# Two experts at fixed places read ahead of routing, a late w_mod batch and five row buffers in a two-layer MoE trunk on one core

## What is computed

```
cs  = silu(c)
mod = cs @ w_mod[i] + b_mod[i]                 # w_mod (2, 1024, 6144)
sh1, sc1, g1, sh2, sc2, g2 = split(mod, 6)
h = rmsnorm(x)*(1+sc1) + sh1
mix = pool_mixer(h)        if i == 0           # windows 2, 4, 8, 16
mix = recurrent_block(h)   if i == 1           # conv of width 4, RG-LRU
x = x + g1 * mix
h2 = rmsnorm(x)*(1+sc2) + sh2
x = x + g2 * moe(h2)       # 16 experts, best group of 4, then its top 2
# moe: silu(h2 @ w_gate[e]) * (h2 @ w_up[e]) * gate, @ w_down[e]; D_FF = 512
y = rmsnorm(x)             # after both layers
```

## Time and profile before

| what | us |
|---|---|
| median of 3 runs | 1042.4 |
| the profiled execution | 1042.29 |
| its span | 1040.5 |
| TensorE busy, share | 867.1 (83%) |
| VectorE busy | 297.9 (29%) |
| ScalarE busy | 199.0 (19%) |
| GpSimd busy | 61.8 (6%) |
| SP's DMA queue, share of 16 engines | 66.3% |
| mean HBM rate over the span | 304 GB/s |

### The profile page before, as it was taken

One profiled execution on the slowest core, in us unless ns is written; L12 is line 12 of the kernel. 1 busy time (PEld: TensorE's weight loads), 2 busy tenths in 40 slices (PEclk: granted clock), 3 DMA queues, 4 the chain that ended last, 5 costly groups with the idle time before them and its releaser, 6 DMA issues.

```text
span 1040.5 us, 14093 instructions
## 1 busy us (share of the span) xinstructions
PE 867.1 (83%) x5770; PEld 446.4 (43%) x5770; DVE 297.9 (29%) x672; ACT 199.0 (19%) x355; POOL 61.8 (6%) x142
## 2 busy tenths in 40 slices
PE   2778777999999998359999999964599999999930
PEld 0433433443333332248887888743244333333210
DVE  2494470110010110363320256065110110010018
ACT  1230511000110000231111851262110000010014
POOL 1000010000011000000000000000101000011000
PEclk9989688999999999659999999967599999999975
DMA  8999989999999999592020000017999999999983
GB/s 272 413 415 422 420 323 418 422 421 420 414 420 420 420 421 375 194 389 86 1 81 1 1 1 1 6 54 277 423 421 406 331 320 408 421 420 420 422 323 145
DMA packets 58834, 311.31 MB, mean 299 GB/s; under 512 B 8173, under 2 KB 11549, under 8 KB 28041
## 3 DMA queue, kind: packets, MB, share of 16 engines
q1 hardware_dynamic: 46416, 278.98, 66.3%
q0 software_dynamic: 6336, 17.83, 4.4%
q10 hardware_dynamic: 6017, 13.58, 3.6%
HBM read 294.68 MB, written 21.28 MB: 304 GB/s over the span
## 4 chain that ended last, share of the span: by engine, by line
PE 69%; DMA 12%; DVE 8%; ACT 3%; issue 1%; SPq 1%; ACTq 0%; PEldq 0%; POOLq 0%; POOL 0%; PEld 0%; DVEq 0%
PE banks L666 27%; PE banks L688 13%; PE banks L862 12%; DMA ring<-in_moe_w_down_dram 5%; PE banks L915 3%; PE banks L907 3%; PE banks L884 3%; PE banks L635 2%; DMA ring<-in_w_mod_dram 2%; ACT hT L989 2%; DMA work<-h_rows,toks 2%; PE banks L589 1%; DVE work L1206 1%; DMA work<-y_rows 1%; SPq L421 1%
## 5 line engine op out<-in xcount | busy, mean ns | idle before, releaser
L666 PE MATMUL banks<-ring,work 128*32 128x512 f32 (+1 forms) x1280 | 240.3, 594 | 2.7 <-DMA hT<-in_moe_w_up_dram 2.7
L688 PE MATMUL banks<-ring,work 128*32 128x512 f32 (+1 forms) x992 | 155.6, 593 | 4.4 <-DMA ring<-in_moe_w_down_dram 4.4
L862 PE MATMUL banks<-hT,ring 128*128 128x272 f32 x512 | 120.8, 398 | 7.4 <-ACTq L365 6.6
L666 PEld LDWEIGHTS banks<-ring,work 128*32 128x32 f32 (+1 forms) x1280 | 72.4, 118 | 115.8 <-issue 113.4
L666 PE MATMUL banks<-work 128*32 128x512 f32 (+1 forms) x592 | 113.6, 594 | 0.8 <-DMA work<-in_moe_w_up_dram 0.8
L862 PEld LDWEIGHTS banks<-hT,ring 128*128 128x128 f32 x512 | 98.5, 193 | 29.3 <-ACTq L365 6.8
L666 PE MATMUL banks<-hT,work 128*32 128x512 f32 (+1 forms) x368 | 92.2, 612 | 1.7 <-DVE work L1549 1.7
L688 PEld LDWEIGHTS banks<-ring,work 128*32 128x32 f32 (+1 forms) x992 | 50.9, 118 | 94.1 <-issue 92.0
L1566 DVE COPY work<-banks 128x512 f32<-128x512 f32 x22 | 15.2, 691 | 218.7 <-PE banks L688 218.7
L553 PE MATMUL banks<-ring,work 128*32 128x512 f32 x384 | 47.9, 638 | 19.4 <-DMA ring<-in_w_mod_dram 19.4
L1558 DVE TENSOR_TENSOR work<-work,banks 128x512 f32<-128x512 f32 x22 | 15.1, 687 | 143.8 <-PE banks L666 143.8
(11 more groups left out here) (256 smaller groups left out, 837.9 us busy)
## 6 DMA issues: line engine op xcount, KB each, us to landing
ring<-in_moe_w_down_dram SPq DMA_DIRECT2D x58, 1024.0 KB, 19.0
ring<-in_w_mod_dram SPq DMA_DIRECT2D x48, 1024.0 KB, 24.1
ring<-in_moe_w_up_dram SPq DMA_DIRECT2D x40, 1024.0 KB, 15.3
ring<-in_moe_w_gate_dram SPq DMA_DIRECT2D x36, 1024.0 KB, 15.4
work<-in_moe_w_up_dram SPq DMA_DIRECT2D x18, 1024.0 KB, 22.5
hT<-in_moe_w_gate_dram SPq DMA_DIRECT2D x14, 1024.0 KB, 16.2
work<-in_moe_w_gate_dram SPq DMA_DIRECT2D x14, 1024.0 KB, 17.9
hT<-in_moe_w_up_dram SPq DMA_DIRECT2D x6, 1024.0 KB, 14.1
```

Of the source, the lines that this page charges most:

```text
L666: last = pe.matmul(bank[part][c0:c0 + cn, :], xe[b][:, k, c0:c0 + cn], w[:, kk, :], start=(k == 0), stop=(k == DC - 1))
L688: last = pe.matmul(bank[2 + half][c0:c0 + cn, :], hidT[b][:, k, c0:c0 + cn], w[:, kk, half * HALF:(half + 1) * HALF], start=(k == 0), stop ...
L862: last = pe.matmul(bank[2 * (i % 2) + h][:, 0:H2], w[:, k, :], hT[:, k, h * H2:(h + 1) * H2], start=(k == 0), stop=(k == DC - 1))
```

## The change

- Experts 0 and 1 leave the ranking and get fixed places 14 and 15 with room for 96 tokens each. These come first in the order of tiles, and their 12 loads (`load_fixed`) wait only for their slots, not for `order_ready`: in layer 0 behind w_mod's fifth batch, in layer 1 during the LRU. The ranked places hold 4, 4, 4, 3 x 5, 2 x 5 and 1 groups of 32.
- w_mod is read in the order 0, 1, 2, 3, 5, 4. Five batches come at the front (`AHEAD`); the sixth is issued by SP after all loads of layer 0's expert stage, into slots 4 to 11, each piece after its slot's last use. Its product stands at the head of the sum of the y rows, on a copy of silu(c) that is kept aside (`silu_kept`). Its gates are cut at the head of VectorE's LRU.
- mod(3) is split around mean(1); mod(4) moves ahead of the transposes of h rows.
- Rows of h and of x have five buffers each in the routing. ScalarE no longer waits for a store to reuse one; the loads into the `work` slots wait for the stores instead.

```diff
-    GROUP_CAPS = [4] * 3 + [3] * 6 + [2] * 7
-    GROUP_OF = [p for p, n in enumerate(GROUP_CAPS) for _ in range(n)]
+    FIXED = 2
+    RANKED = NE - FIXED
+    GROUP_CAPS = [4] * 3 + [3] * 5 + [2] * 5 + [1] + [3] * FIXED
+    PLACE_ORDER = [*range(RANKED, NE), *range(RANKED)]
+    GROUP_OF = [p for p in PLACE_ORDER for _ in range(GROUP_CAPS[p])]
...
+    MOD_ORDER = [0, 1, 2, 3, 5, 4]
+    AHEAD = 5 * SPB
...
-    LOADS = sorted(FIRST_USE, key=lambda u: (FIRST_USE[u], u))
+    FIXED_LOADS = sorted([u for u in FIRST_USE if u[0] >= RANKED], key=lambda u: (FIRST_USE[u], u))
+    RANKED_LOADS = sorted([u for u in FIRST_USE if u[0] < RANKED], key=lambda u: (FIRST_USE[u], u))
+    FIXED_SLOTS = [*range(4, MRING), 2, 3, 0, 1]
...
+    LATE_SLOTS = sorted(range(4, MRING), key=lambda x: LAST_USE[HELD[x][-1]])
+    MOD_SLOT = [u % MRING for u in range(AHEAD)] + LATE_SLOTS
...
-        htok = [ys[0], ys[1]]
+        htok = [work[:, n:n + D] for n in (11264, 15360, 16384, 17408)] + [ys[0]]
...
+            def load_fixed(l):
+                for u in FIXED_LOADS:
+                    p, part, h = u
+                    x = SLOT[u]
+                    if l == 0:
+                        sp.wait_ge(mod_used, MOD_LAST[x])
+                    elif x < 2:
+                        sp.wait_ge(o_added, 2 * DC)
+                    else:
+                        sp.wait_ge(lru_used, max(x // 2 + 1, 4 if x < 4 else 0))
+                    load_piece(l, p - RANKED, 2 * part + h, piece[x], piece_loaded[x])
...
                     else:
                         sp.wait_ge(rt[l]["list_ready"], 2)
+                        for b in range(2):
+                            sp.wait_ge(rt[l][f"rows_stored{b}"], 16 * ((NT + 1 - b) // 2))
                         if l == 0:
-                            sp.wait_ge(mod_done, DEPTH * NBATCH)
+                            sp.wait_ge(mod_done, AHEAD // SPB)
+                        else:
+                            sp.wait_ge(x_rows_stored[1], 16 * (NT - 3))
...
-            load_mod(1, range(NSL))
+            load_mod(range(NSL, AHEAD))
+            load_fixed(0)
             load_moe(0)
             load_overflow(0)
+            load_mod(range(AHEAD, DEPTH * NSL))
             load_second(0)
             load_lru(0)
...
+            load_fixed(1)
             load_moe(1)
...
                 mod_turn(2)
-                mod(3)
-                mod_turn(3)
+                mod(3, range(0, 4))
...
                 sample_logits(l)
+                if l == 0:
+                    mod(4)
...
                 if l == 1:
                     return
+                pe.wait_ge(silu_c, 3)
+                mod(5)
                 for j in range(NT):
+                    if j == 2:
+                        mod_turn(5)
...
                     w = TW[j]
-                    if j >= 2:
-                        act.wait_ge(r[f"rows_stored{j % 2}"], 16 * (j // 2))
...
-                        if j >= 2:
-                            act.wait_ge(x_rows_stored[j % 2], 16 * (j // 2))
```

More of the change, by code:

```diff
@@ L99, in hybrid_trunk_kernel @@
     SLOT = {u: x for x in range(XRING) for u in HELD[x]}
+    LATE_SLOTS = sorted(range(4, MRING), key=lambda x: LAST_USE[HELD[x][-1]])
+    MOD_SLOT = [u % MRING for u in range(AHEAD)] + LATE_SLOTS
+    MOD_LAST = {MOD_SLOT[u]: u + 1 for u in range(AHEAD)}
+    assert len(MOD_SLOT) == DEPTH * NSL
     with ExitStack() as ctx:
@@ L132, in hybrid_trunk_kernel @@
         iota_e = sb("iota_e", [P, NE])
+        fixed_last = sb("fixed_last", [P, NE])
+        silu_kept = sb("silu_kept", [P, DC, NQ])
+        scT = work[:, 12288:12288 + DC * QW].rearrange("p (c n) -> p c n", c=DC)
         row_parts = sb("row_parts", [P, 2, 2 * NT])
@@ L354, in loads_ahead, with mod_loads @@
             if l == 0:
-                return DEPTH * NSL // MRING if x < MRING else 0
-            return loads_ahead(0, x) + len(HELD[x]) + (1 if x < MRING and x % 2 == 0 else 0)
+                return MOD_SLOT[:AHEAD].count(x)
+            return MOD_SLOT.count(x) + len(HELD[x]) + (1 if x < MRING and x % 2 == 0 else 0)
+        def mod_loads(u):
+            x = MOD_SLOT[u]
+            return MOD_SLOT[:u + 1].count(x) + (len(HELD[x]) if u >= AHEAD else 0)
         block = ctx.enter_context(nc.Block())
@@ L396, in _, with load_mod @@
         def _(sp):
[L397 to L402, removed]
+            def load_mod(us):
+                for u in us:
+                    l, b, k = MOD_ORDER[u // SPB] // NBATCH, MOD_ORDER[u // SPB] % NBATCH, u % SPB
+                    x = MOD_SLOT[u]
+                    if u >= AHEAD:
+                        wait_last_use(0, x)
+                    elif u >= MRING:
                         sp.wait_ge(mod_used, u - MRING + 1)
-                    sp.dma_start(piece[u % MRING], w_mod[l][k * P:(k + 1) * P, b * BATCH:(b + 1) * BATCH]
-                                 ).then_inc(piece_loaded[u % MRING], 16)
+                    sp.dma_start(piece[x], w_mod[l][k * P:(k + 1) * P, b * BATCH:(b + 1) * BATCH]
+                                 ).then_inc(piece_loaded[x], 16)
             def wait_used(l, u):
@@ L427, in load_moe @@
                 expert = {}
-                for u in LOADS:
+                for u in RANKED_LOADS:
                     p, part, h = u
@@ L771, in turn_x @@
                             last.then_inc(r["turn"], 1)
-                if l == 0:
-                    mod(4)
-                    mod_turn(4)
-                else:
+                if l == 1:
                     pe.wait_ge(gate_cols_ready, 1)
@@ L929, in _ @@
             mean(1)
+            mod(3, range(4, SPB))
             logits(0)
+            mod_turn(3)
             stage_end(pe, "pe")
@@ L1264, in _ @@
             own(dve.tensor_scalar(row_parts[:, 1, :], row_parts[:, 1, :], quarter[:, 0:1], None, ALU.add))
+            own(dve.tensor_copy(fixed_last[:, :], iota_e[:, :]))
+            for e in range(FIXED):
+                dve.memset(fixed_last[:, e:e + 1], 1e5 * (e + 1))
             own(dve.tensor_copy(invcnt[:, :], iota_e[:, 0:16]))
```

77 lines of the change are left out of this document (41 added, 36 removed).

## The result

| | us |
|---|---|
| before, median of 18 runs | 1043.75 (1041.13 to 1047.37) |
| after, median of 18 runs | 1047.76 (1044.92 to 1052.94) |
| ratio | 1.0042, 95% interval 1.0028 to 1.0056 |

The change makes the kernel 4.4 us slower (0.0042 x 1043.75; the interval is 2.9 to 5.8 us). The forecast was 1051.8 in 1039 to 1060, slower at 0.70: the sign is right and the time 4 us too high; counted as a change, 4.4 us are a little under half of the 9.5 forecast.

A forecast was written before the change was run, and what follows sets the result against it. At the expert stages' ends TensorE and DMA were taken to end together, loads coming every 2.81 us. The terms 1.1 + 3.7 + 11.5 - 10.5 + 3.7 = +9.5 gave 1051.8 us, range 1039 to 1060.

The forecast's parts named there:

- E: The end of the first expert stage, the moment from which the forecast counts the marks up to norm(2).
- A: Front of layer 0: routing later because the row transposes wait behind mod(4), +1.1 us.
- B: Each expert stage: mixed tiles and loads closer at the end make it longer, +3.7 us, counted twice.
- C: First expert stage's end to norm(2): y rows come later behind the late w_mod pieces, +11.5 us.
- D: Second routing: list made 9.5 us earlier, first gather 1 us shorter, -10.5 us, bounds -9.5 and -15.2.
- Rival F: Expert stages: TensorE, not the loads, sets their end, so the kernel gets faster, 1036 us; chance 0.17.
- Rival N: Whole kernel: no change, 1044 us, as the gather is short and y rows lose only their bytes; chance 0.13.

The follow-up runs named there:

- e3: Kernel after with mod(4) back behind the transposes of h rows: 1036.2 us, ratio to before 0.9941.
- e5: Kernel after with the tiles of the three fullest ranked places, one expert each, ahead of the fixed places: 1044.4 us, ratio to before 1.0009.
- e2: Kernel after with all six w_mod batches ahead, mod(5) in layer 0's routing again, fixed slots in ring order: 1037.9 us, ratio to before 0.9960.
- e8: Kernel after with y rows ahead of the late w_mod batch on SP's queue and mod(5) behind the y transposes: 1052.4 us, ratio to before 1.0085.
- e1: Kernel before with only the five buffers for rows of h and of x: 1032.8 us, ratio to before 0.9902.
- e6: Kernel after with layer 1's 12 fixed loads waiting for the ranking: 1057.6 us, ratio to before 1.0141.
- e7: Kernel before with the five row buffers and mod(3) split around the mean, no fixed experts, no late batch: 1028.7 us, ratio to before 0.9863.
- e10: e7 unchanged, run again beside e9 on the same chip: 1028.2 us, ratio to before 0.9851.
- e4: Kernel after with the edits of both e2 and e3: 1039.7 us, ratio to before 0.9968.
- e9: e7 with the change's fixed places and early loads in layer 1 only: 1027.8 us, ratio to before 0.9841.

## Why the prediction was right, and where it was off

**Sign and shape: right.** The transposes start at 125.89 behind the eight w_mod products (forecast 125.0), the first stage is 258.98 us long (259.1), DMA is full from there to the last y row, the first pair is used at E + 21.1 (22.5) and norm(2) starts 10.7 us later after E (11.5), and the list follows VectorE's operands. None of the three signs against it came: no stage of 253 us, no norm(2) within 5 us of its old distance, no waiting list.

**A (+1.1, measured +1.6): right in size, but it hid a loss.** The step said "the whole routing is therefore 1.1 us later, not 7 earlier". It is so in after. That the 7 us were there to be had, 8.1 as e3 measured, made mod(4)'s place the most expensive line of the change beside the late batch.

**B (+3.7 twice, measured +3.6 and +2.7): right.** e5 takes out the mixed tiles and gets 2.5 us back in the first stage where 2.0 were priced. The second stage was 1.0 too dear: its first products take 8.83 us where stage 1 needs 9.99. Both have their weights in place; what differs is the granted clock, 0.50 from 166 to 170 and 0.83 to 176 in stage 1, 0.61 from 745 to 750 and then 1.00 in stage 2.

**C (+11.5, measured +10.7): right.** The gate came at E + 10.2 for a forecast E + 10: the scatter beside a full queue took 8.51 us, the 8.4 of the earlier trace rows. The last w_mod piece, issued at 420.42, landed 23.2 us later, at E + 18.5 (19.3), and the first pair was complete 2.6 us behind it (3.25). Which of its two halves came last the trace can't say, since both count on one semaphore. The share of the other queue can be estimated: by the forecast's count 6.2 us of w_mod were left at the gate, and they took 8.3, so the other queue had about a quarter, where a third was assumed. The Trainium skill, "DMA: Bandwidth & Descriptors", section "Queues, rings and completion order", has engines go round robin between queues; with even halves C would have been about 14, and the trace says 10.7. (In the sum's own terms halves cost 12.4 us in place of 9.3, 3.1 more and not the 2.5 that the forecast gives.) e2 shows that all of C goes when the batch is in front, e8 that norm(2) is late all the same when the y rows come first but TensorE's program still has the batch ahead of it.

**D (-10.5, measured -14.6 and some in the LRU): this is the step that failed, by its size.** The list's 9.5 were right (10.0, and 10.0 again in e1, alone). The gather was put at -1 and measured -4.6. The sentence was "four loads go out at the same moment as the gather". They do not: SP has its two hT loads out by 727.4, waits 13.8 us for the x rows' stores and asks for the four work loads only at 741.36, 3.2 us after the gather was issued, when it has all but landed. That wait is part of the change itself. I had counted how many loads are left and not looked at what stands in SP's queue at the gather's issue. Before, it asks for 14 loads from 710.92 on; at 2.81 us each some eight of them can have landed by 732.98, and the queue is still full. e1, e6, e7 and e10 keep such a queue and have gathers of 10.30, about 10, 10.35 and 10.23 us; after, e2, e3, e4, e5, e8 and e9 read ahead and have 4.26, 4.32, 4.24, 4.29, 4.65, 4.81 and 4.57. The bound of -15.2 was right; the value within it was not. "The 12 early loads themselves save nothing" falls with it: they save nothing in weights, but 4 to 6 us in the latency of what has to pass them.

With D at -14.6 the forecast's own sum would be +5.4, 1.5 us off the trace's 3.9; C, the second B and the LRU make the rest. Rival F (1036) fell, since B and C are as forecast. Rival N, at 1044, is as near in time as the forecast (3.8 us against 4.0): "the gather is short" was right, "the y rows lose only their bytes" was not.

## What to carry to other kernels

- A transfer that has to be short (a gather, a small scatter) is priced by what stands in the queues when it is issued, not by how many loads are still to come: look at the loading engine's own timeline at that moment. And look once more at where the saved time goes; in e9 the next latency-bound transfer took half of it back.
- When DMA is full, moving a batch out of one joint puts it into another. Ask of each joint who waits there: w_mod beside a gather that TensorE waits for anyway was nearly free where the stage starts at 166 (e2), not where it starts at 158 (e4); beside the y rows it cost 10 us. And ask when the values are needed: here the batch was multiplied ahead of a norm that does not use it.
- Try the parts of a change alone. This one loses 4 us as a whole; its two simplest parts alone, more row buffers and a batch split around a norm, win 15 to 16 (e7, e10), and fixed experts in layer 1 add nothing that can be told from zero to that (e9).

## What the runs showed of the hardware

- The same indirect gather of one tile: 4.2 to 4.8 us where at most two loads of 1 MB were asked for in the 20 us before it, 8.9 to 10.4 us where a dozen were, in the second routing of twelve traces. The scatter that carries y rows: 3.2 us alone, 8.5 to 8.6 with w_mod pieces ahead of it on another queue (after, e3, e5, e6). In these traces a transfer beside a full queue pays 4 to 6 us more, whichever its direction.
- SP's own issues take longer when many loads are out: in e6 four loads take 2.09 us to issue, the last four of the twelve 7.17, two more 9.38. What holds them was not tested.
- A wait of TensorE costs more than its length: in e4, behind 8.9 us without weights, the granted clock is 0.54 for 5 us and 32 products take 5.78 us, the next 32 take 3.57.
- In e4 the gate weights need 29.22 us from issue to landing and in e6 33.01, and the loads ahead of them account for it: at 2.81 us per load that is 10 to 12 loads, about what SP had out.
